# Sums of squares for three latent norms: one ones-product on TensorE per norm, blocks added on GpSimd

## What is computed

```python
def _rms_norm(x, g):
    xf = x.astype(F32)
    y = xf * lax.rsqrt(jnp.mean(xf * xf, axis=-1, keepdims=True) + EPS)
    return (y * g.astype(F32)).astype(x.dtype)
...
    q = (_rms_norm(cq, q_norm_g) @ w_uq).reshape(bsz, seq, MLA_HEADS, MLA_NOPE_DIM + MLA_ROPE_DIM)
...
    kv = (_rms_norm(ckv, kv_norm_g) @ w_ukv).reshape(bsz, seq, MLA_HEADS, MLA_NOPE_DIM + MLA_V_DIM)
...
        y = jnp.concatenate([_rms_norm(y_hy, gn[:g0]), _rms_norm(y_lr, gn[g0:g1]),
                             _rms_norm(y_at, gn[g1:])], axis=-1)
```

## Time and profile before

| | |
|---|---|
| median of 3 executions | 1650.45 us (1649.51 to 1651.31) |
| profiled execution | 1650.62 us |
| its span | 1648.6 us |
| TensorE busy | 1544.1 us, 94% |
| VectorE busy | 1049.0 us, 64% |
| ScalarE busy | 711.8 us, 43% |
| GpSimd busy | 350.0 us, 21% |

### The profile page before, as it was taken

The page is one execution under the profiler, slowest core; times in us unless marked ns, Lnnn a source line. Parts: engine busy times, 40 slices in busy tenths (PEclk is TensorE's granted clock), DMA queues, the critical chain, the costliest instruction groups (busy, mean ns, idle before and its releaser), DMA issues.

```text
span 1648.6 us, 15488 instructions
## 1 busy us (share of the span) xinstructions
PE 1544.1 (94%) x5758; PEld 1035.5 (63%) x5758; DVE 1049.0 (64%) x1024; ACT 711.8 (43%) x686; POOL 350.0 (21%) x190
## 2 busy tenths in 40 slices
PE   6999999999999999999998993399999999999997
PEld 3444587743344445555566882388888888888774
DVE  4532236425431655666755656599999999999886
ACT  3210000134411213443432342277777777777773
POOL 0031000000000001233535534011224322233204
PEclk9999999999999999999999995699999999999998
DMA  9311210224000000000031338499999999999995
GB/s 320 109 51 51 89 65 0 55 49 94 25 0 1 0 0 26 1 0 26 26 102 41 115 102 308 170 349 374 378 378 378 379 368 379 378 378 379 370 378 206
DMA packets 152884, 284.40 MB, mean 173 GB/s; under 512 B 25300, under 2 KB 35874, under 8 KB 152835
## 3 DMA queue, kind: packets, MB, share of 16 engines
q1 hardware_dynamic: 147219, 263.28, 45.0%
q0 software_dynamic: 4464, 16.25, 3.8%
q10 hardware_dynamic: 1152, 4.19, 0.7%
HBM read 259.07 MB, written 24.64 MB: 172 GB/s over the span
## 4 chain that ended last, share of the span: by engine, by line
PE 83%; DVE 6%; DMA 4%; ACT 3%; issue 2%; SPq 0%; POOL 0%; POOLq 0%; ACTq 0%; DVEq 0%
PE psum L1089 13%; PE psum L1496 9%; PE psum L1498 9%; PE psum L1497 9%; PE psum L1374 6%; PE psum L1310 4%; PE psum L1157 3%; PE psum L1070 3%; DMA arena<-in_exp_w_down 3%; PE psum L1280 2%; PE psum L1035 2%; PE psum L1420 2%; PE psum L1422 2%; PE psum L1421 2%; PE psum L1173 2%
## 5 line engine op out<-in xcount | busy, mean ns | idle before, releaser
L1948 DVE TENSOR_TENSOR split_at<-arena,split_at 128x2048 fp32r<-128x2048 f32 x188 | 427.8, 2290 | 61.5 <-ACT split_at L951 60.7
L951 ACT ACTIVATE split_at<-arena 128x2048 fp32r<-128x2048 f32 x192 | 367.3, 1915 | 64.9 <-PE psum L1498 53.2
L1496 PE MATMUL psum<-split_at,split_at 128*128 128x512 f32 x768 | 306.1, 399 | 1.4 <-DVE split_at L1954 1.4
L1498 PE MATMUL psum<-split_at,split_at 128*128 128x512 f32 x768 | 300.5, 391 | 0.0
L1497 PE MATMUL psum<-split_at,split_at 128*128 128x512 f32 x768 | 299.8, 390 | 0.0
L1089 PE MATMUL psum<-arena 128*128 128x512 f32 (+1 forms) x544 | 242.8, 600 | 2.4 <-DVE arena L1753 2.4
L1089 PEld LDWEIGHTS psum<-arena 128*128 128x128 f32 (+1 forms) x544 | 100.6, 188 | 139.0 <-issue 138.9
L1498 PEld LDWEIGHTS psum<-split_at,split_at 128*128 128x128 f32 x768 | 144.7, 188 | 31.2
L1496 PEld LDWEIGHTS psum<-split_at,split_at 128*128 128x128 f32 x768 | 144.9, 189 | 29.8 <-DVE split_at L1954 1.8
L1497 PEld LDWEIGHTS psum<-split_at,split_at 128*128 128x128 f32 x768 | 145.0, 189 | 28.4
L1374 PE MATMUL psum<-arena 128*128 128x512 f32 x256 | 120.8, 594 | 6.2 <-ACT arena L860 5.4
(11 more groups left out here) (285 smaller groups left out, 2206.4 us busy)
## 6 DMA issues: line engine op xcount, KB each, us to landing
arena<-in_exp_w_gate SPq DMA_DIRECT2D x64, 1024.0 KB, 14.4
arena<-in_exp_w_up SPq DMA_DIRECT2D x64, 1024.0 KB, 14.2
arena<-in_exp_w_down SPq DMA_DIRECT2D x64, 1024.0 KB, 14.4
arena<-in_w_in SPq DMA_DIRECT2D x9, 1024.0 KB, 8.5
arena<-in_x SPq DMA_DIRECT2D x8, 512.0 KB, 6.5
xhat_scratch<-arena SPq DMA_DIRECT2D x8, 512.0 KB, 10.0
arena<-in_w_out SPq DMA_DIRECT2D x8, 512.0 KB, 3.6
arena<-xhat_scratch SPq DMA_DIRECT2D x8, 512.0 KB, 5.0
```

What stands on the lines that cost most here:

```text
L951: a(flat(wsplit[c % WS][0]), wraw[:, c], ACT.Copy).then_inc(s_whi, 1)
L1496: mm(bank(out_bank), src[0][:, k, :], whi[:, k % 4, :], start=(k == 0), stop=False)
L1498: ins = mm(bank(out_bank), src[1][:, k, :], whi[:, k % 4, :], start=False, stop=(k == KT - 1))
L1948: tt(flat(lo), wraw[:, c], flat(hi), ALU.subtract).then_inc(s_wlo, 1)
```

## The change

ScalarE now squares the blocks of a norm alternately: the first into a new accumulator `sqa`, every further one into `sq`. GpSimd adds `sq` to `sqa` in place (`add_squares`), seven additions in all. TensorE multiplies ones by `sqa` once per norm: three pairs of matmuls where there were ten. The squares wait for additions rather than for TensorE. `sqa` lies where `rb_lru`, the root of the last norm, is written later.

In the lists some places move with it. The product for `ckv` now stands behind the first half of `gates(2)`. The product for `cq` stands behind three `values`, the one for the recurrence behind the eighth. ScalarE copies three `values` before the root for `cq` and squares both recurrence blocks right after it. To free a semaphore or two, three loads now count on semaphores that other loads have used (`s_rw`, `s_gff`); nothing is issued in another place for that.

```diff
+            def add_squares(n, done):
+
+                pool.wait_ge(s_sq, n + 1)
+                pool.tensor_tensor(sqa, sqa, sq, ALU.add).then_inc(s_sqa, 1)
+                pool.wait_ge(s_sqa, done)
+
+            add_squares(1, 1)
+            for n in range(3, 8):
+                add_squares(n, n - 1)
+            add_squares(9, 7)
...
             def squares(i, n):
 
                 act.wait_ge(s_pj, i + 1)
-                if n:
-                    act.wait_ge(s_ssq, n)
-                a(sq, bank(proj_bank(i), 2), ACT.Square).then_inc(s_sq, 1)
+                if n == 2:
+                    act.wait_ge(s_ssq, 1)
+                if n >= 3:
+                    act.wait_ge(s_sqa, n - 2)
+                a(sqa if n in (0, 2) else sq, bank(proj_bank(i), 2), ACT.Square).then_inc(s_sq, 1)
...
             act.wait_ge(s_rb, 1)
-            rms_root(rb, 8, QL)
-            values_copy(0)
+            for t in range(3):
+                values_copy(t)
+            rms_root(rb, 2, QL)
             lru_squares(0)
-            values_copy(1)
-            values_copy(2)
             lru_squares(1)
...
-            def sum_squares(n, first, last):
-
-                if n == 2 or n == 8:
-                    pe.wait_ge(s_rsd, 1 if n == 2 else 2)
-                pe.wait_ge(s_sq, n + 1)
+            def sum_squares(n):
+
+                pe.wait_ge(s_sqa, (1, 6, 7)[n])
+                if n:
+                    pe.wait_ge(s_rsd, n)
                 for j in range(2):
-                    ins = mm(bank(2 + j), ones, sq[:, HALF * j:HALF * j + HALF], start=first, stop=last)
+                    ins = mm(bank(2 + j), ones, sqa[:, HALF * j:HALF * j + HALF], start=True, stop=True)
                 ins.then_inc(s_ssq, 1)
...
-            project(I_KV + 1, 2, 4)
-            sum_squares(0, True, False)
-            project(I_KV + 1, 4, 6)
+            project(I_KV + 1, 2, 6)
             gates(1, 1)
             project(I_KV + 1, 6, 8)
-            project(I_KR, 0, 2)
-            sum_squares(1, False, True)
-            project(I_KR, 2, 5)
+            project(I_KR, 0, 4)
             gates(2, 0)
+            sum_squares(0)
+            project(I_KR, 4, 5)
...
             project(I_CQ + 1, 1, 8)
-            sum_squares(2, True, False)
             for c in range(2, 6):
                 project(I_CQ + c)
-                sum_squares(1 + c, False, False)
...
-            values(0)
-            sum_squares(7, False, True)
-            values(1)
-            values(2)
-            sum_squares(8, True, False)
-            values(3)
-            values(4)
-            sum_squares(9, False, True)
-            for t in range(5, TT):
+            for t in range(3):
                 values(t)
+            sum_squares(1)
+            for t in range(3, TT):
+                values(t)
+            sum_squares(2)
```

More of the change, by code:

```diff
@@ L191, in encoder @@
         kr = mem(48080, T)
-        sq = mem(49104, T)
+        sq, sqa = mem(49104, T), mem(8144, T)
         yT_hy = mem(50128, 2, T)
@@ L259, in encoder @@
         s_gmm, s_gact, s_lact, s_lv, s_hsg = sem("gates_psum"), sem("gates_read"), sem("lru_act"), sem("lru_dve"), sem("lru_gated")
-        s_sq, s_ssq, s_rsd, s_rb = sem("squares"), sem("squares_summed"), sem("rms_root"), sem("rms_applied")
+        s_sqa, s_sq, s_ssq, s_rsd, s_rb = sem("squares_added"), sem("squares"), sem("squares_summed"), sem("rms_root"), sem("rms_applied")
         s_mw, s_rope, s_krm, s_kro = sem("mla_w_ld"), sem("rope_ld"), sem("kr_partner_psum"), sem("kr_roped")
@@ L273, in encoder @@
         s_wo, s_woh, s_wol = [sem(f"w_out_ld{i}") for i in range(2)], sem("w_out_high"), sem("w_out_split")
-        s_gb, s_rw, s_gff = sem("gains_ld"), sem("router_w_ld"), sem("ffn_gains_ld")
+        s_gb = sem("gains_ld")
+        s_rw, s_gff = s_rope, s_mw
         s_xh = [sem(f"xhat_ld{i}") for i in range(2)]
@@ L355, in encoder @@
         SUMS = 10
+        ROWS = 3
         ROOTS = 3
@@ L649, in _ @@
             finish(NE - 2, (NE - 2) % 4, False)
-            pool.wait_ge(s_gff, 48)
+            pool.wait_ge(s_gff, 16 * 16 + 48)
             for i in range(TT):
@@ L793, in lru_squares @@
                 act.wait_ge(s_hsg, c + 1)
-                act.wait_ge(s_ssq, 8 + c)
-                a(sq, hs[:, c, :], ACT.Square).then_inc(s_sq, 1)
+                act.wait_ge(s_ssq, 2)
+                a(sq if c else sqa, hs[:, c, :], ACT.Square).then_inc(s_sq, 1)
             gates(0)
@@ L800, in _ @@
             squares(I_KV + 1, 1)
-            rms_root(rb, 2, KVL)
+            rms_root(rb, 1, KVL)
             gates(2)
@@ L818, in _ @@
                 values_copy(t)
-            rms_root(rb_lru, 10, LRW)
+            rms_root(rb_lru, 3, LRW)
             def heads_copy(u):
@@ L912, in heads_root @@
             def heads_root(i):
-                act.wait_ge(s_ssq, SUMS + i + 1)
+                act.wait_ge(s_ssq, ROWS + i + 1)
                 a(asd[:, i:i + 1], bank(7)[:, i:i + 1], ACT.Sqrt, scale=1.0 / (NH * DV), bias=eps).then_inc(s_rsd, 1)
@@ L1404, in logits @@
                 if i == 0:
-                    pe.wait_ge(s_rw, 16)
+                    pe.wait_ge(s_rw, 48 + 16)
                 if i:
@@ L1970, in expert @@
                     if c == 8 and last:
-                        v.wait_ge(s_gff, 48)
+                        v.wait_ge(s_gff, 16 * 16 + 48)
                         link(v.tensor_copy(idxf_t[:, 0:1], idx_t[:, NE - 1:NE]))
```

## The result

The changed kernel took 1636.11 us (median of 4 runs, 1635.01 to 1636.71) against 1649.98 for the kernel before (4 runs, 1649.47 to 1651.31). The ratio is 0.9914, with a 95% interval of 0.9897 to 0.9931. (Ratios are estimated over the single executions, so they can differ from the quotient of two medians in the third decimal.) The medians are 13.9 us apart, and the interval stands for 11.4 to 17.0; the prediction's sum was 11.1 and its time 1639.5. The sign, the place and nearly every gap were as forecast. So the time alone would have pointed to the wrong case; which case it is, only the trace tells.

A forecast was written before the change was run, and what follows sets the result against it. TensorE was taken to bound the kernel, 83% of the span. Front 6.0, collision -2.3, clock -1.0, middle 6.9 and tail 1.5 sum to 11.1 us off 1650.62: 1639.5, range 1636.0 to 1642.5.

The forecast's parts named there:

- Sign and mechanism: Faster, chance 0.95: seven of ten sum pairs leave TensorE, 12.0 us of matmuls, not all where TensorE was the limit.
- Case (a), the collision: GpSimd's addition goes first at the last cq scan, holding VectorE back 2.3; 1639.5, own range 1637.8 to 1641, chance 0.45.
- Cases (b) to (e): The four rivals; the one between (c) and (e): four middle pairs only filled a wait, 6.9 lost, 1646.4, chance 0.05.
- (b): No collision on the chain: the middle addition misses the boundary and harms nothing; 2.3 come back, 1637.2, chance 0.26.
- (e): Slower: GpSimd's addition sets the pace for all three sums; 1654 if an addition takes 10 us; chance 0.02.
- (c): VectorE keeps its turn: front addition waits behind the scan, gap 2.0; nothing lost in the middle; 1640.1, chance 0.17.
- Front, 6.0: Up to second half of gates(2), 6.0 us earlier: pair 1.7, gap 2.4, clock behind it 1.7, rounding and matmul widths 0.2.
- Middle, 6.9: Blocks of cq: four sums between later blocks come off whole, 4 x 1.72 = 6.9 us; the one inside a wait brings nothing.
- Tail, 1.5: values to the heads: one of three sums goes, 1.7 less, with 0.2 taken off; 1.5, bounds 0.7 to 1.7.
- The clock: Behind the grown gap before the third cq block, 1.0 us more lost than before, between 0 and 1.7.

The follow-up runs named there:

- The middle undone: Changed kernel with cq summed by six products again, no additions for it; ckv and recurrence stay changed: 1639.56 us, ratio 0.9936 to the kernel before.
- The front undone: Changed kernel with ckv summed by two products again, the second at its old place; other two norms stay changed: 1640.36 us, ratio 0.9950.
- the later addition: Changed kernel with GpSimd's cq additions waiting until VectorE has read the first cq block: 1634.04 us, ratio 0.9907 to the kernel before.
- the repeat: The changed kernel again, unedited, beside the kernel before: 1635.97 us, ratio 0.9918.
- the run with two additions: Changed kernel with each GpSimd addition done twice, the second releasing the sum: 1643.98 us, ratio 0.9971 to the kernel before.

## What the prediction had right, and the step that was mis-sized

**Sign and mechanism: right.** Three pairs are left, no gap ahead of the first, and the blocks behind the third one close up. The middle undone costs 3.6 at the median, 4.2 to 5.0 by the traces, and the prediction's terms for it give 6.9 - 2.3 - 1.0 = 3.6. The front undone costs 4.4, where the prediction has 6.0. The step that failed is the clock's: what the low clock costs behind a gap was read from one trace as if it belonged to the gap. The runs showed 0 or 1.6 us behind the same gap of 2.4, 1.8 to 2.8 behind the same 4.1 at the rotary partner, and 0.3 to 0.5 more than before in the middle where the sum had 1.0.

**Case (a), the collision: right, a little too dear.** "So the gap grows to 4.1 + 2.3 = 6.4 us": it is 6.12, and the product takes 3.24, not 3.5. Moving the addition away takes 2.0 off the gap, and 1.9 off the time. Cases (b) to (e) are out for this kernel; a gap of 4.1 as in (b) is what the later addition made of it, and came out at 1634.0. For (c) the prediction named the rule of the Trainium skill (SBUF — State Buffer, "Who interferes with whom") that the first to issue has its turn. Here the addition begins at 454.19 and L1755 at 454.40, so the rows fit that rule and give (a).

**Front, 6.0: right for the trace it was read from** (6.15), but not for the kernel. Of it, 1.7 was the low clock behind a gap of 2.4 us, and that loss is in two of three traces of before and not in the third, nor in the one with the front undone. Without it the front is worth 4.5. So it is partly luck that 6.0 fits the first pair of traces. One trace can't say this by itself.

**Middle, 6.9: right.** Third block to `values` is 6.5 less, and the four blocks take 57.06 to 57.22 where 4 x 13.74 = 54.96 would be full clock.

**Tail, 1.5: right** (1.6).

**The clock: the term that was mis-sized.** The prediction took 1.0 more of loss in the middle than before, and no change at the rotary gap, which it let move "gap and clock loss included". The middle lost 2.1 to 2.3 where before lost 1.8, so 0.3 to 0.5. And the rotary gap, unchanged in length, lost 1.8 in one trace and 2.5 in the other where before lost 2.8. In the first trace these two are worth 0.7 + 1.0 = 1.7 of the 2.2 us by which the sum was short in this stretch; the rest is 0.3 from the collision and 0.2 from front and tail. Whether the smaller loss at the rotary gap is chance stays open. All four traces with two products for `ckv` take 11.36 to 11.42 from the rotary partner to the gates, and all seven with one product that have the gap take 10.35 to 11.10, so the change may have a part in it, which the prediction put at nothing.

**The base.** The sum was taken off 1650.62, one profiled execution, and the kernel before is slower there than it is at large. Its medians in the later runs were 1647.7 to 1648.4. Against those, the changed kernel's 1636.0 is 11.7 to 12.4 less, and not 13.9. The ratios are less kind to this account: 0.9918 in the repeat stands for 13.5, with an interval of 10.7 to 16.3. So how much of the miss belongs to the base is not settled; the sum of 11.1 is within that interval. Set against one another from `gates(1,1)` on, with 1.7 for the pair ahead, the three traces of before and the two of after differ by between 154.5 - 145.4 + 1.7 = 10.8 and 156.1 - 144.5 + 1.7 = 13.3. The sum of 11.1 lies in that. For the two profiled executions, 15.6 apart, what lies beyond the sum of 11.1 is 1.7 of clock in the stretch, 1.3 in the first 33 us, 1.0 behind the heads and outside the span, and only 0.5 in the prediction's other terms.

**Left open.** Why the first matmuls take 8.5 us in one execution and 10.0 in another; the granted clock doesn't settle it, since a window over them reads 0.83 in the faster of the two and 1.00 in the trace of 10.11. TensorE's own durations say that it ran at a lower rate for longer in the slower: the eight small records just ahead take 1.97 there and 1.09 in the faster, and sixteen records like these take 7.03 at 31.34 in the faster and at 34.30 in the trace. Whether the change has any part in it is open too; a trace of before reached `gates(1,1)` at 389.26, with a sum more ahead of it than the changed kernel's 389.21, so chance would do. The 0.3 to 0.8 by which the stretch from the heads to the end differs weren't followed either.

## What to carry over

A sum that leaves a list was worth its own length here where it stood between busy neighbours, nothing where it stood in a wait, and more than the gap it closed where the clock fell behind that gap. What the clock costs behind a gap should be read from several traces before it goes into a sum: here it was 0 or 1.6 behind the same 2.4 us. An addition handed to GpSimd cost VectorE 2.0 us where it met a two-input operation: look what stands behind VectorE at the moment it is asked for, and delay it by one wait if that is the chain. And what a change frees, here two PSUM banks, may be worth more than the change: with them the same kernel went from 1636 to 1628, and only then did filling the earlier gap pay, down to 1622; without them it gave 1636.

## What the runs showed of the hardware that I had not expected

- The same kernel differed by 4.5 us between two profiled executions, and by 4.6 already where the heads start: 3.1 from the first 33 us and 1.6 behind a gap of 2.4 us, behind which the granted clock was 1.00 in one and 0.81 in the other.
- Turns between VectorE and GpSimd alternated in the places looked at where both waited: in the run with two additions, first addition, scan (4.32 instead of 2.29), second addition (4.20 instead of 2.34). Neither engine got two instructions in a row there while the other waited.
- A memset on GpSimd of the same size, 0.95 us, beside the same two products cost VectorE nothing (2.29 and 1.22).
- A loss of clock doesn't grow with the gap by any rule that I could read: behind 4.1 us in the middle 1.4 to 1.6 were lost, behind 6.12 between 2.1 and 2.5, behind 11.20 (57.38 for four blocks) 2.4.
